# The sums of token blocks move from VectorE to GpSimd, and layer 2's keys are scaled for latent blocks alone

## The reference

```python
for l in range(2):                                   # DEPTH
    x = x + 0.5 * g1 * swiglu(modulate(x, nw[0], sh1, sc1), ffn1_up[l], ffn1_down[l])
    ctx = ctx + 0.5 * cg1 * swiglu(modulate(ctx, nw[0], ch1, cs1), ffn1_up[l], ffn1_down[l])
    hc = modulate(ctx, nw[1], ch2, cs2)
    if last:                                         # layer 2: context gives states alone
        s_f, s_b = context_states(hc @ w_in[l][:, :OFF_Q], lp)
    else:
        ...                                          # the whole mixer and a second FFN on ctx
    yx, _ = token_mixer(modulate(x, nw[1], sh2, sc2), True, s_f, s_b, lp)
    x = x + g2 * yx
    x = x + 0.5 * g3 * swiglu(modulate(x, nw[2], sh3, sc3), ffn2_up[l], ffn2_down[l])
return rmsnorm(x, final_norm_w)

def swiglu(h, w_up, w_down):                         # w_up 1024 x 5632, w_down 2816 x 1024
    a, b = jnp.split(h @ w_up, 2, axis=-1)
    return (jax.nn.silu(a) * b) @ w_down
```

```python
k_t = kc * jnp.exp(-b)          # the key factors
att = jnp.where(mask, jnp.einsum('bhncd,bhnmd->bhncm', q_t, k_t), 0.0)
kv  = jnp.einsum('bhncd,bhnce->bhnde', kc * jnp.exp(b_last - b), vc)
```

## Time and profile before

| | before |
|---|---|
| median of 3 runs | 2830.38 us (2829.36 to 2835.23) |
| the profiled execution | 2831.64 us |
| its span, first to last instruction | 2829.4 us |
| mean granted clock of TensorE | 0.997 |
| TensorE busy | 98% |
| VectorE busy | 1962.4 us, 69% |
| ScalarE busy | 34% |
| GpSimd busy | 19% |

### The profile page before, as it was taken

How to read it: one execution, slowest core, us unless ns; L and a number is a source line. 1 busy time by engine, 2 the same in 40 slices (tenths; PEclk the granted TensorE clock), 3 DMA queues, 4 the chain that set the end, 5 groups by cost and what they waited for, 6 DMA issues and landing times.

```text
span 2829.4 us, 40890 instructions
## 1 busy us (share of the span) xinstructions
PE 2784.5 (98%) x15744; PEld 2472.1 (87%) x15744; DVE 1962.4 (69%) x3220; ACT 975.0 (34%) x1543; POOL 532.4 (19%) x456
## 2 busy tenths in 40 slices
PE   7999999999999999999999999999999999999998
PEld 5899899888888888999999889898988778888886
DVE  4668889565367747988886788888856577563334
ACT  5233224354322233423233433242444332432223
POOL 1013113214500020213132213131331500200000
PEclk9999999999999999999999999999999999999999
DMA  7322433231134423233332323424223145343332
GB/s 244 103 60 81 130 105 86 69 77 45 41 94 124 122 65 101 83 105 107 102 110 83 97 72 89 126 80 131 80 58 91 42 131 153 107 132 104 92 96 79
DMA packets 463787, 275.56 MB, mean 97 GB/s; under 512 B 17610, under 2 KB 461812, under 8 KB 463604
## 3 DMA queue, kind: packets, MB, share of 16 engines
q1 hardware_dynamic: 461396, 269.09, 33.8%
q10 hardware_dynamic: 2208, 4.00, 0.4%
HBM read 270.95 MB, written 2.10 MB: 97 GB/s over the span
## 4 chain that ended last, share of the span: by engine, by line
PE 92%; DVE 3%; ACT 2%; issue 1%; DMA 1%; POOL 0%; SPq 0%; ACTq 0%; DVEq 0%; POOLq 0%
PE ps L1698 37%; PE ps L1712 19%; PE ps L1956 17%; PE ps L1963 9%; PE ps L1924 2%; PE ps L1744 2%; PE ps L1929 1%; PE ps L1039 1%; DMA wraw<-in_ffn_up 1%; PE ps L1019 1%; ACT whi L2054 1%; DVE wlo L2357 0%; ACT hhi L2119 0%; PE ps L1007 0%; DVE hlo L2499 0%
## 5 line engine op out<-in xcount | busy, mean ns | idle before, releaser
L2357 DVE TENSOR_TENSOR wlo<-wraw,whi 128x1024 fp32r<-128x1024 f32 (+2 forms) x299 | 320.3, 1076 | 259.5 <-ACT whi L2054 256.6
L2054 ACT ACTIVATE whi<-wraw 128x1024 fp32r<-128x1024 f32 (+2 forms) x291 | 269.1, 926 | 588.2 <-PE ps L1712 403.4
L1698 PE MATMUL ps<-hhi,whi 128*128 128x512 f32 x1472 | 461.2, 364 | 2.2 <-ACT whi L2054 2.2
L1698 PE MATMUL ps<-hlo,whi 128*128 128x512 f32 x1472 | 453.1, 359 | 0.0
L1712 PE MATMUL ps<-hhi,wlo 128*128 128x512 f32 x1472 | 318.4, 362 | 0.0
L1698 PEld LDWEIGHTS ps<-hhi,whi 128*128 128x128 f32 x1472 | 245.9, 189 | 48.6 <-ACT whi L2054 3.8
L1712 PEld LDWEIGHTS ps<-hhi,wlo 128*128 128x128 f32 x1472 | 244.1, 188 | 44.6 <-issue 3.2
L1698 PEld LDWEIGHTS ps<-hlo,whi 128*128 128x128 f32 x1472 | 245.4, 188 | 42.8 <-issue 0.5
L2989 POOL TENSOR_TENSOR ssum<-wraw 128x512 f32<-128x512 f32 x52 | 73.1, 1406 | 1014.4 <-PE ps L1963 367.5
L1698 PE MATMUL ps<-mhi_fast,whi 128*128 128x512 f32 (+1 forms) x912 | 236.3, 340 | 1.4 <-DVE mlo_fast L2814 1.4
L1698 PE MATMUL ps<-mlo_fast,whi 128*128 128x512 f32 (+1 forms) x912 | 234.6, 338 | 0.0
(11 more groups left out here) (310 smaller groups left out, 5709.6 us busy)
## 6 DMA issues: line engine op xcount, KB each, us to landing
wraw<-in_ffn_up SPq DMA_DIRECT2D x176, 512.0 KB, 4.2
wraw<-in_w_in SPq DMA_DIRECT2D x64, 512.0 KB, 4.1
wraw<-in_ffn_down SPq DMA_DIRECT2D x80, 384.0 KB, 4.5
wraw<-in_w_mod SPq DMA_DIRECT2D x68, 256.0 KB, 3.1
modraw<-in_w_mod SPq DMA_DIRECT2D x32, 512.0 KB, 3.7
modraw_down<-in_w_mod SPq DMA_DIRECT2D x30, 512.0 KB, 3.7
flow_first<-in_w_mod SPq DMA_DIRECT2D x86, 128.0 KB, 4.2
first_mod<-in_w_mod SPq DMA_DIRECT2D x8, 1024.0 KB, 12.0
```

The costliest lines, as they stand in the source:

```text
L1698: nc.tensor.matmul(o, whi[:, slot, k, :], a[:, k * NT + t0:k * NT + t0 + n], start=(k == 0 and a is hi), stop=False)
L2054: nc.scalar.activation(whi[:, slot2, k, n], wraw[:, slot4, k, n], ACT.Copy).then_inc(hi_split, 1)
L2357: ins = nc.vector.tensor_tensor(wlo[:, slot2, k, n], wraw[:, slot4, k, n], whi[:, slot2, k, n].bitcast(F32), ALU.subtract)
```

## The change

Three things are edited. `t_sums` leaves VectorE's queue; a function of the same name on GpSimd issues the same four operations in one chain, after the norm's chunks and before the weight sums. They wait for ScalarE's shift and for the norm, and so stand in the first up group. `t_los` on VectorE takes its four roundings in the first two pairs of the down phase in all three FFNs, and each also waits for the sums that read the block which it overwrites. In layer 2 kt is formed for 512 columns.

```diff
@@ key_factors (ScalarE)
-                nc.scalar.activation(kt[:, d, :], bsum[:, 2 * pr + d, :], ACT.Exp, scale=-1.0 / TAU).then_inc(ekt_ready, 1)
+                nc.scalar.activation(kt[:, d, 0:c], bsum[:, 2 * pr + d, 0:c], ACT.Exp, scale=-1.0 / TAU).then_inc(ekt_ready, 1)
@@ scale_keys (VectorE)
             dve.wait_ge(ekt_ready, 4 * l + 2 * pr + d + 1)
-            nc.vector.tensor_tensor(kt[:, d, :], kq[:, pr, :], kt[:, d, :], ALU.mult)
+            nc.vector.tensor_tensor(kt[:, d, 0:nb * P], kq[:, pr, 0:nb * P], kt[:, d, 0:nb * P], ALU.mult)
@@ VectorE
-            def t_sums(ph, which):
-                f0 = fast_ffn(ph) - 1
-                dve.wait_ge(raw_shifted, DC * (f0 + 1))
-                dve.wait_ge(h_ready[1], DC * (3 * ph["layer"] + 2 * ph["ffn"] + 1))
...
-                    nc.vector.tensor_tensor(out, x0, x1, op).then_inc(t_summed, 1)
-                    dve.wait_ge(t_summed, 4 * f0 + n + 1)
-
             def t_los(ph, which):
                 for n in which:
                     dve.wait_ge(t_hi, 4 * (fast_ffn(ph) - 1) + n + 1)
+                    dve.wait_ge(t_summed, 4 * (fast_ffn(ph) - 1) + (3, 2, 4, 4)[n])
...
-                            if fast and makes_t(ph) and short(ph):
-                                t_los(ph, (3,))
...
                             if makes_t(ph):
-                                if 2 * i + h < 2:
-                                    t_sums(ph, (4 * i + 2 * h, 4 * i + 2 * h + 1))
-                                t_los(ph, (((), (0,), (1, 2), ()) if short(ph) else ((), (0, 1), (2, 3), ()))[2 * i + h])
+                                t_los(ph, ((0, 1), (2, 3), (), ())[2 * i + h])
@@ GpSimd
+            def t_sums(ph):
+                f0 = fast_ffn(ph) - 1
+                pool.wait_ge(raw_shifted, DC * (f0 + 1))
+                pool.wait_ge(h_ready[1], DC * (3 * ph["layer"] + 2 * ph["ffn"] + 1))
+                s22, s12, s11, s21 = fast_blocks(hraw[:, 0:DC // 2 * NT], hraw[:, DC // 2 * NT:])
+                for out, x0, x1, op in ((s22, s12, s22, ALU.subtract), (s12, s11, s12, ALU.subtract),
+                                        (s11, s22, s11, ALU.subtract), (s21, s11, s21, ALU.add)):
+                    t_steps.link(nc.gpsimd.tensor_tensor(out, x0, x1, op))
+
+            t_steps = Steps(pool, t_summed)
             odd_chunks(0, BOTH)
             for ph in plan:
                 fast_sums(ph)
+                if makes_t(ph):
+                    t_sums(ph)
```

More of the change, by code:

```diff
@@ L754, in fast_next @@
         return nxt if nxt["fast"] else None
-    def short(ph):
-        return groups_of(ph["layer"], ph["ffn"])[ph["third"]][1] <= DC // 2
     def makes_t(ph):
```

## The result

| | before | after |
|---|---|---|
| median | 2832.23 us, 6 runs (2829.36 to 2835.23) | 2847.36 us, 6 runs (2846.09 to 2850.58) |
| profiled execution | 2831.64 us | 2846.90 us |
| its span | 2829.4 us | 2845.1 us |
| mean granted clock | 0.997 | 0.995 |

The ratio is 1.0055, with a 95% interval of 1.0044 to 1.0065. Of 2830.4 us that is 15.6 us more, where 14.1 were forecast. The predicted 2844.5 lies 2.9 us under the measured median, inside the range of 2834 to 2850.

What follows compares the result with a forecast made beforehand. TensorE's matmul stream, busy for 98% of the span, was taken as the bound. Stops of 2.0 + 6.3 + 6.3 less 0.5 for the keys gave +14.1 us on 2830.4, so 2844.5 us, range 2834 to 2850.

Steps and rivals of the forecast that it cites:

- Removal worth nothing: Down groups of three FFNs: taking twelve sums, 21.1 us, off VectorE gains 0, since TensorE hardly waits there.
- Length of a sum: GpSimd addition of 1536 elements, extrapolated from 512 and 768: 3.5 us, between 2.8 and 4.0.
- First FFN: First up group: sums hold mlo_fast, then wlo; TensorE stops for about 2.0 us at 71.94 us, range 0 to 2.6.
- Second and third FFN: First up groups: VectorE lags 10.7 us at the second pair, less 4.4 slack; TensorE stops 6.3 us in each.
- the first meeting: Second FFN, about 1073 us: first sum holds the last of eight products, delaying mtmp_fast and whi; TensorE stops 3.4 us.
- L: Forecast length of one GpSimd sum, 3.5 us, and the most that each meeting can hold a VectorE operation.
- the 0.2 for pauses: Second FFN: 0.2 us for GpSimd's own pauses, added to three holds of 3.5 us, giving 10.7 us of lag.
- The prediction's rule: VectorE operations with both tensors in SBUF wait until GpSimd's operation is over, alternating; those reading PSUM aren't held.
- The clock: Rival 3, heavier: a low-clock stretch after a 3 us stop in all three FFNs adds 5.1 us, 2849.6; chance 0.08.
- The keys: Layer 2's attention: forming kt for the latent blocks alone gains 0.5 us, between 0 and 1.4.
- GpSimd yields: Rival 1: sums slip into VectorE's pauses, lag stays under 4.4 us, no loss; 2829.9 us, chance 0.12.
- the loss is lighter: Rival 2: L is 2.8 or one of three meetings misses; +7.9 us, 2838.3 us, chance 0.11.

Runs made afterwards that it cites:

- the sums on VectorE: Changed kernel, but the four sums stand on VectorE in the first up group's second pair, ahead of its mtmp_fast; 2838.34 us, ratio 1.0030.
- sixteen short sums: Changed kernel with each of the four sums per FFN cut into four pieces of 384 columns on GpSimd, in one chain; 2845.39 us, ratio 1.0051.
- the kernel with one sum per pair: Against before: keys shortened, four sums on GpSimd, the second to fourth each waiting for a pair's end in the first up group; 2832.52 us, ratio 1.0001.

## Why the prediction was right, point by point

- **Removal worth nothing.** Right. The window of the first FFN's down group, after, against the first row:

```profile
142.00:194.00 52.00, 52.00 (x302) 45.16 (x302) 25.09 (x33) 14.20 (x16) 4.39 (x3) 1.00 0.24 69
```

VectorE is busy for 25.09 us in place of 30.42, and TensorE for 52.00 as before. In the two other down groups TensorE's delay changes by +0.3 and 0.0 us, so none of its small waits there came back. The 21 us of VectorE's work bought nothing.
- **Length of a sum.** 3.5 us was forecast. Alone it is 3.50 to 3.53 (the shortest 3.497), worked out from two rows at 512 and 768 columns. In the chain the median is 4.13, since a sum also waits for VectorE's operation ahead of it, up to 0.8 us. What VectorE lost didn't grow by it: three holds of 3.2 to 3.3 us each.
- **First FFN.** 2.0 us forecast, a step of 1.7 measured, with the order forecast: mlo_fast held, then wlo.
- **Second and third FFN.** 6.3 us each forecast, 5.5 and 5.4 measured. The step that failed is the first meeting. The first sum did not hold the last product: it was issued at 1074.01, and the eight products still took 3.25 us. So mtmp_fast and the whi behind it weren't late at the first pair, and the 3.4 us of stop forecast there did not come; TensorE's wait there went from 0.31 to 0.41 us. The stop came whole at the second pair, 0.9 us for the wlo at 1094.17 and the rest for whi. Three holds came all the same, because the sums then met only one operation each: wlo was held for 3.2 us and the two tensor_scalar for 6.6. That is 9.8 of lag where 10.7 stood in the sum: each hold was 0.2 to 0.3 us shorter than L, and the 0.2 for pauses didn't come. TensorE's waits for whi rose by 8.7 us, where some 12 were forecast.
- **What is held.** The prediction's rule was that an operation with both tensors in SBUF is held. It said nothing of tensor_scalar, with one, and two thirds of the lag came from the two of them. The number didn't suffer: had they passed, the third and the fourth sum would by the same rule have met products. That is argued, not measured.
- **The clock.** It was a rival with 0.08 for three FFNs and 1.7 us each. It came in two of three, with 1.6 us each: 3.2 us that the sum lacked. Across the kernels it was the companion of nearly every long stop. The text's argument against it, that 3 us are short, was wrong: it came with stops of 2.0 to 5.5 us, though not with the third FFN's stop of 2.6 with the sums on VectorE, nor with the 1.5 us at 72 us.
- **The keys.** -0.5 us forecast, -0.5 measured.
- **Sum.** -0.3 - 0.8 - 0.9 for the stops and +3.2 for the clock make +1.2 of the difference between 14.1 and the 15.7 of the spans. That the 2.0 too much for the stops and the 3.2 left out for the clock leave so little is luck; the cause of the stops and the three up groups in which they stand are not. The first loads gave +0.8, the stretch of the earlier trace rows that is missing after -1.5, and small steps +1.1; these belong to the executions, not to the change.
- **The rivals.** That GpSimd yields happened once each in the second and the third FFN, for the first sum, and then no longer. That the loss is lighter, by a missed meeting, did not come, since the sums that follow found others to hold.

## What to carry to other kernels

An engine that is 19% busy isn't free to take work from one that is 69% busy when they share a way into memory: count the operations of the second that fall beside the first and read two SBUF tensors, and its tensor_scalar too, up to one for each operation of the first, and add nearly that operation's length for each. Then compare that lag with the slack at the place where the bound engine needs the result; under it the move costs nothing, above it the excess is paid in full, and in nine of the ten stops of 2 us or more here a low clock was paid as well. If the work must move, put one piece beside operations that here kept their times (those that read PSUM, a transpose, a reduction) and let the other engine catch up before the next, as the kernel with one sum per pair does; but first ask whether the freed engine was waited for, which here it was not.

## What the runs showed of the hardware

- A GpSimd copy of 128x1536 float32 takes 1.47 us, a fill 1.38, and an addition or subtraction with two inputs 3.50.
- Beside fills a VectorE tensor_scalar of 256 columns is held (2.57 us for two in place of 0.61), while two-tensor operations aren't. Beside GpSimd sums, which read and write, two of them took 7.18 us.
- VectorE's operation issued before the GpSimd one has begun goes first, and with operations back to back even the one behind it can: at 1074.01 the first sum took 4.08 us in place of 3.50, and no product was lengthened. Later each engine had one operation in turn.
- Ten stops of TensorE of 2.0 to 5.5 us came with nine stretches of a few us at a lower granted clock (0.50 to 0.72 in windows of 2 us), which cost 1.4 to 2.6 us each. In four of the nine the clock fell before the stop had ended: with sixteen short sums it is 0.59 from 1096 to 1098 us, where TensorE does nothing until 1099.3. Of two equal stops of 2.65 us in one execution only one had it, and what decides is open.
